# Recurrent mixer: substitution columns nine and later on GpSimd beside VectorE, first scores behind the second condition block, condition halves reloaded in another order

## What is computed

```
def _rwkv7_scan(r, w, k, v, kh, a):
    def step(state, inp):
        r_t, w_t, k_t, v_t, kh_t, a_t = inp
        removed = jnp.einsum('zhvk,zhk->zhv', state, kh_t)
        state = (state * w_t[:, :, None, :] - removed[..., None] * (kh_t * a_t)[:, :, None, :]
                 + v_t[..., None] * k_t[:, :, None, :])
        return state, jnp.einsum('zhvk,zhk->zhv', state, r_t)
    _, y = lax.scan(step, jnp.zeros((z, h, n, n), jnp.float32), seq)
```

## Time and profile before

| | us |
|---|---|
| runs | 2075.38, 2076.01, 2080.68 |
| median | 2076.01 |
| span of the profiled execution | 2073.7 |
| TensorE busy in it | 1972.9 (95%) |
| VectorE / ScalarE / GpSimd busy | 735.4 / 407.7 / 39.4 |

### The profile page before, as it was taken

The page is one execution under the profiler, slowest core; times in us unless marked ns, Lnnn a source line. Parts: engine busy times, 40 slices in busy tenths (PEclk is TensorE's granted clock), DMA queues, the critical chain, the costliest instruction groups (busy, mean ns, idle before and its releaser), DMA issues.

```text
span 2073.7 us, 34414 instructions
## 1 busy us (share of the span) xinstructions
PE 1972.9 (95%) x15174; PEld 1327.4 (64%) x15174; DVE 735.4 (35%) x1576; ACT 407.7 (20%) x802; POOL 39.4 (2%) x41
## 2 busy tenths in 40 slices
PE   6999988899999999999899999999998999999998
PEld 3554766787554555445475888888877876463564
DVE  2694588564311111111234245423673420000001
ACT  3200263232311111111235300003232120000001
POOL 0000211000000000000000000000000000000000
PEclk9999997799999999999999999999999999999999
DMA  9710005106799999999766369753310059999992
GB/s 366 253 41 0 1 1 201 47 14 266 294 429 424 429 430 430 428 428 431 291 248 246 98 248 360 271 221 124 124 39 2 1 202 376 399 410 405 413 402 103
DMA packets 162337, 512.91 MB, mean 247 GB/s; under 512 B 9070, under 2 KB 32413, under 8 KB 149533
## 3 DMA queue, kind: packets, MB, share of 16 engines
q1 hardware_dynamic: 146720, 481.18, 58.8%
q10 hardware_dynamic: 15485, 29.77, 3.8%
HBM read 509.88 MB, written 1.05 MB: 246 GB/s over the span
## 4 chain that ended last, share of the span: by engine, by line
PE 88%; DVE 4%; DMA 3%; issue 2%; ACT 1%; SPq 1%; DVEq 0%; POOL 0%; ACTq 0%; POOLq 0%
PE PS L389 26%; PE PS L2572 11%; PE PS L2596 5%; PE PS L2408 4%; PE PS L2487 3%; PE PS L2698 3%; PE PS L2498 3%; PE PS L2690 3%; PE PS L2775 2%; PE PS L396 2%; PE PS L3282 2%; PE PS L2702 2%; DMA work<-in_moe_w_gate_up_dram 1%; PE PS L2778 1%; PE PS L2117 1%
## 5 line engine op out<-in xcount | busy, mean ns | idle before, releaser
L389 PE MATMUL PS<-hT,work 128*128 128x256 f32 x1408 | 313.4, 382 | 1.2 <-issue 1.2
L389 PEld LDWEIGHTS PS<-hT,work 128*128 128x128 f32 x1408 | 266.7, 191 | 43.8 <-issue 7.9
L2572 PE MATMUL PS<-work,sq 128*64 128x512 f32 x1024 | 222.6, 592 | 0.0
L389 PE MATMUL PS<-work 128*128 128x256 f32 (+1 forms) x544 | 177.1, 486 | 0.0
L2572 PEld LDWEIGHTS PS<-work,sq 128*64 128x64 f32 x1024 | 76.6, 137 | 143.2 <-issue 142.4
L389 PEld LDWEIGHTS PS<-work 128*128 128x128 f32 x544 | 103.0, 190 | 73.5 <-issue 65.7
L2596 PE MATMUL PS<-work 128*64 128x512 f32 x512 | 113.4, 595 | 10.0 <-issue 8.6
L2596 PEld LDWEIGHTS PS<-work 128*64 128x64 f32 x512 | 36.8, 137 | 76.3 <-issue 74.4
L2690 PE MATMUL PS<-work,sq 128*64 128x512 f32 (+1 forms) x384 | 80.2, 576 | 5.6 <-DMA work<-in_moe_w_gate_up_dram 5.5
L2640 DVE TENSOR_TENSOR work<-work,PS 128x64 f32<-128x64 f32 x128 | 18.2, 216 | 184.9 <-PE PS L2572 184.9
L2408 PE MATMUL PS<-work 128*128 128x256 f32 x352 | 76.3, 379 | 0.0
(11 more groups left out here) (656 smaller groups left out, 2640.8 us busy)
## 6 DMA issues: line engine op xcount, KB each, us to landing
work<-in_ex_gate_dram SPq DMA_DIRECT2D x32, 2048.0 KB, 12.6
work<-in_ex_up_dram SPq DMA_DIRECT2D x32, 2048.0 KB, 15.0
work<-in_ex_down_dram SPq DMA_DIRECT2D x32, 2048.0 KB, 11.1
work<-in_moe_w_gate_up_dram SPq DMA_DIRECT2D x32, 2048.0 KB, 13.1
work<-in_moe_w_down_dram SPq DMA_DIRECT2D x16, 2048.0 KB, 16.2
work<-in_ada_w_dram ACTq DMA_DIRECT2D x14, 2048.0 KB, 11.0
work<-in_moe_w_gate_up_dram SPq DMA_DIRECT2D x16, 1536.0 KB, 15.3
work<-in_ada_w_dram SPq DMA_DIRECT2D x10, 2048.0 KB, 10.3
```

The lines of the kernel that those rows point to most:

```text
L389: ins = pe.matmul(outp, lhs, rhs, start=n == 0, stop=n == len(pairs) - 1, **kw)
L2572: ins = pe.matmul(PS[pair[m], 6 + j, :], xs[:, k, pair[m]], unit(U[name] + 3 * m + j, KT, F)[:, k, :], start=k == 0, stop=k == KT - 1)
```

## The change

- The substitution is split by column of `PX`. VectorE keeps columns 0 to 8 in every step (`SUB_DVE = 9`); columns 9 and later are done by a second loop on GpSimd, `rw_later_columns_pool`, with 22 steps (s = 9 to 30) of 2 instructions, each linked to the one in front. Its product buffer lies in `Gs`. It runs behind the clearing of `UV` and ahead of the clearing of `XTall`.
- TensorE waits, ahead of L1818, for GpSimd's last step too.
- The first scores stand behind the halves of block 7 instead of ahead of block 6.
- `HALVES` uses place 3 a second time: the old list was 1 2 3 0 1 2 0 1 2 0 1 2.
- The mask of the first scores stands after step 20 of the substitution and waits for `ada_half` >= 7, since place 3 holds half 6 by then.

```
-    HALVES = [1, 2, 3, 0] + [(h - 3) % 3 for h in range(4, 2 * (N_ADA1 - N_RW))]
+    HALVES = [1, 2, 3, 0, 1, 2, 3, 0, 1, 2, 0, 1]
...
         pool.wait_ge(S["rw_nt"], NCH + 2)
+        rw_later_columns_pool()
         po.link(pool.memset(XTall[quad(0, 1), :, 0:B32], 0.0))
...
-        for d in range(2):
-            rw_sc_pe(0, d)
         for n in range(N_RW, N_ADA1):
             ada_halves_pe(n)
+            if n == N_RW + 1:
+                for d in range(2):
+                    rw_sc_pe(0, d)
...
         pe.wait_ge(S["rw_id"], 7)
+        pe.wait_ge(S["pool_step"], later_columns_done[0])
...
-            m = B32 - 1 - s
-            t = outer[:, 0:2 * m * (s + 1)].rearrange("p (t b j) -> p t b j", t=m, b=2)
-            dv.link(dve.tensor_tensor(t, along(PN.rearrange("p b t s -> p t b s")[:, s + 1:, :, s], s + 1),
-                                      over(PX[:, s, :, 0:s + 1], m), ALU.mult))
-            part = PX[:, s + 1:, :, 0:s + 1]
-            ins = dve.tensor_tensor(part, part, t, ALU.add)
+            ins = substituted(dve, dv, outer, s, 0, min(s + 1, SUB_DVE))
             if s < B32 - 2:
                 dv.link(ins)
-            if s == 16:
-                dve.wait_ge(S["ada_half"], 4)
+            if s == 20:
+                dve.wait_ge(S["ada_half"], 7)
                 rw_mask_dve(0, 0)
...
+    SUB_DVE = 9
+    later_columns_done = [0]
+
+    def substituted(eng, chain, buf, s, j0, j1):
+
+        m = B32 - 1 - s
+        t = buf[:, 0:2 * m * (j1 - j0)].rearrange("p (t b j) -> p t b j", t=m, b=2)
+        chain.link(eng.tensor_tensor(t, along(PN.rearrange("p b t s -> p t b s")[:, s + 1:, :, s], j1 - j0),
+                                     over(PX[:, s, :, j0:j1], m), ALU.mult))
+        part = PX[:, s + 1:, :, j0:j1]
+        return eng.tensor_tensor(part, part, t, ALU.add)
+
+    def rw_later_columns_pool():
+
+        pool.wait_ge(S["rw_ready"], 3)
+        pool.wait_ge(S["rw_id"], 6)
+        pool.wait_ge(S["rw_ia"], 14)
+        buf = Gs.rearrange("p d n -> p (d n)")
+        for s in range(SUB_DVE, B32 - 1):
+            po.link(substituted(pool, po, buf, s, SUB_DVE, s + 1))
+        later_columns_done[0] = po.n
```

## The result

The changed kernel takes 2079.2 us (median of 20 runs, 2074.54 to 2085.55) where the kernel before, in 20 runs beside it, takes 2076.53 (2070.88 to 2082.06). The ratio is 1.0022, with a 95% interval of 1.0013 to 1.0031: slower by about 4.6 us, 2.7 to 6.4. (The ratio on record is larger than that of the two medians, which lie 2.7 us apart, and of the two means, 3.3 apart; all three say that the change is slower.) That is inside the 0.3% I called "no change", and inside the range, but on the other side of the 2076 than the forecast of 2070.0. The interval excludes the forecast.

A forecast was written before the change was run, and what follows sets the result against it. TensorE was taken to bound the start of L1818, VectorE 1.7 us behind. Moving it from 376.44 to 370.4 gains 6.0 us, passed through in full: 2076.0 - 6.0 = 2070.0 us (own range 2066.5 to 2072; overall range 2065.0 to 2082.0).

The forecast's parts named there:

- What bounded the kernel, and TensorE's side: Mixer ahead of L1818: TensorE holds the transposes; with scores moved and loads earlier it is ready at 370.4, not 376.44.
- my two values: TensorE ready for L1818 after the last half and two turns: 371.1 at the lower clock, 369.2 at the upper.
- The other case: TensorE's clock stays at the upper level, also through L1818, saving up to 2.8 us there: gain near 9; chance 0.04 beyond 9.
- the order changes, the loads don't: Rival: condition loads land no earlier, TensorE stays the bound, the offload is worth nothing: 2076; counted within the second rival's 0.32.
- VectorE's and GpSimd's own costs: Substitution loops: VectorE 27.1 us with mask, ending 366.3; GpSimd's 44 instructions 28.0 us, ending 367.3; 264 elements 0.74 us.
- What two engines do to each other: VectorE and GpSimd loops both reading SBUF: no mutual slowdown assumed, from L1433 running unheld inside GpSimd's L1600.
- The second rival: The loops slow each other, or GpSimd is slow by itself: 2073.5 to 2081.2 us, near 2076; chance 0.32.
- its first form: GpSimd gets no data while VectorE streams and ends its loop at 381.6, 5.2 us later than before.
- the gate: Start of TensorE's transposes L1818, which open the way to the scan; at 376.44 before, forecast 370.4.
- Taking turns: Rival: VectorE and GpSimd instructions alternate, loops end at 394.3, gate 17.9 us late, 2093.9 us; chance 0.18.
- A gain or a loss at the gate goes through in full: Everything behind the start of L1818 shifts with it to the kernel's end, so 6.0 us there is 6.0 in all.

The follow-up runs named there:

- e10: The change with GpSimd's 44 two-input instructions replaced by one-input copies of the same sizes, later columns' products and sums left out; 2074.91 us, one run.
- e9: The change with one more wait, so VectorE's loop starts only when GpSimd's is done; 2097.04 us, one run.
- e3: The change without GpSimd's loop and the wait for it, columns nine and later left out; 0.9996 of the kernel before.
- e11: The kernel before once more, unchanged; 1.0008 of the kernel before, 0.9994 to 1.0022.
- e1: The kernel before with the change's order of scores, list of halves and mask, whole substitution on VectorE; 1.0015 of the kernel before.
- e5: The kernel before with only the first scores moved, old list and mask; 0.9999 of the kernel before.
- e8: e7 with TensorE's wait for the down weights put ahead of its wait for `hid_moe1`; 1.0006 of the kernel before.
- e12: The change with halves listed 1 2 3 0 three times and the mask behind step 28; 0.9997 of the kernel before.
- e14: The change once more, on the same chip as e15; 1.0033 of the kernel before, median 2081.62 us.
- e15: e12 once more, the change with three halves in each place, on e14's chip; 1.0003 of the kernel before, median 2074.83 us.
- e6: The kernel before with only the new list of halves and its mask behind step 20; 1.0014 of the kernel before.
- e16: The kernel before plus one always-met register wait with another constant, behind the wait for `hid_moe1` in each expert round; 1.0038 of the kernel before.
- e2: The kernel before with only the split at column nine and its wait, old order, list and mask; 1.0012 of the kernel before.
- e7: The kernel before with scores moved, halves listed 1 2 3 0 three times, mask behind step 28; 1.0002 of the kernel before.

## Why the prediction went wrong

**What bounded the kernel, and TensorE's side: right.** TensorE was ready at 371.7 for 370.4 (between 369.2 and 371.1 in the sum); half 11 landed at 366.2 for 366.0; the scores took 1.93 us for 1.9. The clock stayed at its lower level in the turns, so the 371.1 of my two values was the right one. The other case is seen in e10, where the turns at the upper level took 1.88 us instead of 3.51 and the transposes behind them 4.05 instead of 6.20, 2.2 us less where my sum had "up to 2.8". The reload chain did start earlier and landed earlier, and the rival "the order changes, the loads don't" falls.

**VectorE's and GpSimd's own costs: right.** 27.0 and 27.5 us alone for 27.1 and 28.0. The choice of the 512-element row with its two different inputs as the base was good: 264 elements took 0.68 and 0.73, for 0.74.

**What two engines do to each other: the step that failed.** The forecast set this at zero on the strength of one row, L1433 beside GpSimd's L1600. The row was read rightly and was the wrong row: L1600 has one input, and two inputs on GpSimd cost VectorE's 396-element instruction 0.36 to 0.37 us on top of 0.57, one input 0.07 (e10). The row did not show even the 0.07: the L1433 inside L1600 took its 0.68 like the others; why is not shown. The second rival, that they slow each other, is what happened, and more evenly than its first form had it: GpSimd ended at 371.1 and not at 381.6, and VectorE, which that form left alone, at 376.8. Its time, near 2076, was right for the mixer: the gate moved by 0.5 us. That the measured 2079.2 also lies in this rival's 2073.5 to 2081.2 is luck, since the loss comes from a list that the rival doesn't speak of.

**Taking turns: refuted, and priced rightly.** Turns would have put the gate at 394.3. e9 runs the two loops one after the other, gets 394.22, and is 18 us slower than the change (2097.04 us, one run). Side by side they take 37.6 us. The Trainium skill (SBUF — State Buffer, section "Who interferes with whom") has such a pair exclude each other, the one that starts first holding the ports to its end. The runs differ: instructions overlap and stretch, 0.57 to 0.94 and 0.70 to 0.88 us, and the direction of the rule, against this change, was right. It also gives GpSimd's one-input instructions the same hold on VectorE, which e10 doesn't show.

**"A gain or a loss at the gate goes through in full": right in the mixer, and not the whole account.** e3 keeps 4.9 of 5.2 us to the mixer's end (4.2 against e11's), e9 its 17.3 to the end. The small gains of 1.6 us (e1, e5 to e8) are at 0.7 to 3.0 us at the mixer's end, and in no timed ratio. What I never looked at is who else reads the list I saw changed. `HALVES` is counted by every later wait on its places, and its counts set how many registers TensorE computes in a round of the expert loop. The prediction gave the edit as one of loads only; the cost was 2.0 us in the profiled rounds, and by e12, e14 and e15 all of the timed loss, of which more than the rounds' part isn't explained.

**What stays open.** The rounds show 2.0 us where the timed runs lose 2.9 to 6.8 by the list (e6; the difference of the medians of e14 and e15), and 3.6 of the 7.9 in e16. The profiles have a further loss behind the loop. The stretch from 1506 to 2067 us takes 560.6 us in the profile of before and 563.3 in the change, but also 561.1 in e11 and 564.8 in e15, whose timed runs are alike, and 567.9 in e16. Waits for weights are a small part of it: for L2690, in the change L2710, they are 5.5 and 6.6 us in all. The difference lies in one piece of some 52 us, from 1569 to 1621 in the kernel before, in which hardly a DMA runs. The same work there (length, busy and count of TensorE, weight loads, VectorE, ScalarE, GpSimd, granted clock, DMA share, GB/s) in before, e11, the change and e16:

```profile
1568.90:1621.10 52.20, 49.37 (x810) 43.61 (x809) 18.05 (x23) 11.38 (x17) 0.00 (x0) 0.97 0.01 2
1565.40:1617.90 52.50, 49.33 (x810) 43.62 (x809) 18.05 (x23) 11.39 (x17) 0.00 (x0) 0.97 0.01 2
1569.90:1624.30 54.40, 50.97 (x809) 44.86 (x808) 18.04 (x23) 11.37 (x17) 0.00 (x0) 0.94 0.01 2
1569.10:1628.70 59.60, 55.81 (x810) 48.79 (x809) 18.05 (x23) 11.38 (x17) 0.00 (x0) 0.83 0.01 2
```

VectorE and ScalarE are the same to 0.02 us; TensorE takes longer as its granted clock is lower. The 7.4 us between before and e16 here are all of the 7.3 between their stretches, and e15 (56.3 us here, granted clock 0.88) has 4.1 of its 4.2 here as well. The clock differs between two executions of one program too: 0.94 in the change and 0.91 in e14, 0.91 in e12 and 0.88 in e15, so a single profile can't say whether an edit moves it. In the timed runs only the mean granted clock of the whole is on record. Among the 22 runs of the kernel before beside e16, one with a mean clock lower by 0.001 is some 1.2 us longer. The 11 runs of e16 have 0.9727 in the mean and those 22 have 0.9751; by that slope, an estimate, 3 us of the 7.9 go with the clock, and with the 3.6 of the rounds the sum is within the interval. For e14 (0.9746, and 0.9758 beside it) the same estimate gives 1.3 of its 6.8, and some 3.5 stay unplaced. Whether the new code lowers the clock or the executions happened to differ is not shown. e2 also stays unclear: 1.0012, with nothing in its mixer or rounds to account for it, and the interval begins at 1.

## What to carry to other kernels

Before moving elementwise work to GpSimd beside a busy VectorE, count the inputs: with two on both sides VectorE lost 10.5 us for the 8.4 that it was relieved of, beside GpSimd's copies, with one, it lost a sixth of that; and a row that overlaps with one-input work tells nothing of two. When an edit changes how often a shared place is loaded, look at every wait that counts those loads: unequal counts put a register computation in a loop far away, and a list with equal counts cost nothing here. A gate that opens 1.6 us earlier (e5, e7) is below what 10 or 12 timed runs can show, so judge such an edit by its stretch and the whole by the time. And before reading the difference of two profiles' ends as the edit's, compare the granted clock of the same stretch in both.

## What the runs showed of the hardware that I had not expected

- VectorE and GpSimd, both with two inputs, stretch each other without stopping: VectorE's 396-element instruction from 0.57 to 0.94 us, GpSimd's 264-element one from 0.70 to 0.88. The loops went from 27.1 to 37.6 us and from 27.5 to 31.6. VectorE, the faster, pays more.
- The cost grew faster than GpSimd's share, in the two splits tried: 0.95 ns on VectorE for each GpSimd element at 3876 elements, 1.3 at 8096.
- By the reading of the source above, a second register computation behind a wait costs TensorE 0.14 us in each round (29.34 to 29.48), on a kernel that is 95% TensorE; the same two with one wait more cost about 0.12 on top (e16, 29.61), and the first costs 0.05 (e8, 29.29).
- The same 810 matmuls behind the loop take 52.2 us at a granted clock of 0.97 and 59.6 at 0.83, and the granted clock there differs by 0.03 between two executions of one program (e12 and e15).
- Moved behind busy work, 32 small matmuls took 1.93 us for 3.68, at the upper clock; the transposes took 4.05 us at 1.00 where TensorE had not stopped (e10) and 6.20 at 0.55 where it had.
